# 27 of 35 weight units of two layers multiplied as high and low parts

## What is computed

```
def first_block(x, ...):
    for layer in range(DEPTH):                       # two layers
        h = _rmsnorm(x, norm_g[layer])
        if layer % 2 == 0:
            proj = jnp.einsum('bsd,de->bse', h, e_w_in[i])   # 1024 x 3584
            u_val, u_gate, z_a, q_b, k_b, v_b, z_b = _split(proj, EVEN_SIZES)
            ...
        else:
            proj = jnp.einsum('bsd,de->bse', h, o_w_in[i])
            (q_c, kc_, vc_, ks_, vs_, kw_, vw_, g_c, z_c, q_d, k_d, v_d, z_d) = _split(proj, ODD_SIZES)
            ...
        x = x + jnp.einsum('bse,ed->bsd', y, w_out[layer])
    return x
```

## Time and profile before

| what | value |
| --- | --- |
| time, three runs | 1030.06, 1030.6, 1036.0 us (median 1030.6) |
| the profiled execution | 1030.22 us, of which 1028.4 us are the span of the profile |
| granted TensorE clock, mean | 0.976 |
| PE, busy share | 93% |
| DVE, ACT, POOL, busy share | 35%, 40%, 43% |
| layers 0 and 1 | about 0 to 401 us |
| POOL's first subtraction | 370 us |

### The profile page before, as it was taken

The page is one execution under the profiler, slowest core; times in us unless marked ns, Lnnn a source line. Parts: engine busy times, 40 slices in busy tenths (PEclk is TensorE's granted clock), DMA queues, the critical chain, the costliest instruction groups (busy, mean ns, idle before and its releaser), DMA issues.

```text
span 1028.4 us, 15967 instructions
## 1 busy us (share of the span) xinstructions
PE 957.8 (93%) x6896; PEld 874.2 (85%) x6896; DVE 363.5 (35%) x734; ACT 408.1 (40%) x588; POOL 446.0 (43%) x101
## 2 busy tenths in 40 slices
PE   4999889999898798999999998999999979999996
PEld 4887677788676377999999998999999979999996
DVE  4677521320556626640111113222115643341002
ACT  3111541013576423234343444667533545553330
POOL 0000000000000031787766665766787767886780
PEclk9999899999899999999999998999999989999998
DMA  9632245858524363565534443444544625453531
GB/s 353 257 123 82 83 175 205 329 176 316 196 83 164 124 246 126 175 242 183 185 131 158 158 150 111 160 161 152 177 164 164 238 95 200 168 199 130 204 121 41
DMA packets 27470, 177.51 MB, mean 173 GB/s; under 512 B 2904, under 2 KB 5476, under 8 KB 6920
## 3 DMA queue, kind: packets, MB, share of 16 engines
q1 hardware_dynamic: 25960, 174.28, 46.9%
q10 hardware_dynamic: 1440, 2.20, 0.7%
HBM read 174.88 MB, written 3.43 MB: 173 GB/s over the span
## 4 chain that ended last, share of the span: by engine, by line
PE 84%; DVE 10%; ACT 3%; issue 1%; DMA 1%; POOL 0%; DVEq 0%; ACTq 0%
PE proj L571 18%; PE proj L596 14%; PE proj L597 14%; PE proj L598 14%; PE proj L628 3%; PE proj L630 3%; PE proj L629 3%; PE proj L780 3%; PE proj L617 2%; PE transposed L702 2%; PE proj L810 2%; PE mixed L731 1%; PE scores L690 1%; DVE parts L1561 1%; PE scores L677 1%
## 5 line engine op out<-in xcount | busy, mean ns | idle before, releaser
L521 POOL TENSOR_TENSOR w_lo<-raw,w_hi 128x2048 fp32r<-128x2048 f32 x71 | 329.0, 4639 | 269.7 <-ACT w_hi L1050 269.6
L596 PE MATMUL proj<-parts,w_hi 128*128 128x256 f32 x768 | 222.2, 289 | 6.5 <-DVE parts L1383 4.2
L597 PE MATMUL proj<-parts,w_lo 128*128 128x256 f32 x800 | 227.5, 284 | 0.0
L598 PE MATMUL proj<-parts,w_hi 128*128 128x256 f32 x768 | 218.3, 284 | 0.0
L1050 ACT ACTIVATE w_hi<-raw 128x2048 fp32r<-128x2048 f32 x71 | 135.5, 1909 | 99.4 <-PE proj L598 63.8
L596 PEld LDWEIGHTS proj<-parts,w_hi 128*128 128x128 f32 x768 | 148.1, 193 | 8.1 <-issue 5.2
L597 PEld LDWEIGHTS proj<-parts,w_lo 128*128 128x128 f32 x800 | 154.2, 193 | 0.8 <-issue 0.7
L598 PEld LDWEIGHTS proj<-parts,w_hi 128*128 128x128 f32 x768 | 148.0, 193 | 0.0
L525 POOL MEMSET probT<- 128x512 f32 x1 | 0.5, 525 | 247.8 <-PE proj L897 247.8
L571 PE MATMUL proj<-h,raw 128*128 128x256 f32 x320 | 76.5, 403 | 3.0 <-DVE h L1391 3.0
L571 PEld LDWEIGHTS proj<-h,raw 128*128 128x128 f32 x320 | 64.7, 204 | 14.2 <-issue 4.5
(11 more groups left out here) (273 smaller groups left out, 1940.5 us busy)
## 6 DMA issues: line engine op xcount, KB each, us to landing
raw<-in_weights SPq DMA_DIRECT2D x113, 1024.0 KB, 4.9
arena<-in_weights SPq DMA_DIRECT2D x36, 1024.0 KB, 5.0
probT<-in_weights SPq DMA_DIRECT2D x8, 1024.0 KB, 5.7
dil_lines<-dil_line SPq DMA_DIRECT2D x1, 2304.0 KB, 12.1
dil_bias<-dil_lines SPq DMA_DIRECT2D x1, 1536.0 KB, 9.6
xT<-in_x SPq DMA_DIRECT2D x2, 512.0 KB, 5.6
arena<-in_alibi SPq DMA_DIRECT2D x1, 1024.0 KB, 20.6
arena<-in_swa SPq DMA_DIRECT2D x1, 1024.0 KB, 7.3
```

The lines of the kernel that those rows point to most:

```text
L521: nc.gpsimd.tensor_tensor(lo_slots[RAW_AT[n]][:, 0:kt * w], raw_slots[RAW_AT[n]][:, 0:kt * w], hi_slots[HI_AT[m]][:, 0:kt * w].bitcast(F32 ...
L596: nc.tensor.matmul(dst, whi, h, start=first, stop=False)
L597: nc.tensor.matmul(dst, wlo, h, start=False, stop=False)
L598: last = nc.tensor.matmul(dst, whi, lo[:, k, :], start=False, stop=stop)
```

## The change

Of the 35 units of layers 0 and 1, 27 are now split: all but uv0, ug0, bq1, bk0, bk1, bv0, bv1 and kcvc. For these ACT makes 27 more high copies, and POOL subtracts each in two halves, with one signal behind the second; from rq0 on it subtracts whole units as before. POOL's work for zb0 and what follows waits for `conv_done`, the end of DVE's convolution. The norms of x0 and x1 write whole activations to `h0` and `h1` (`wide`) and then parts: eight ACT copies and eight DVE subtractions each. The attention outputs are split ahead of wo0 and wo1 (`operand_high` on ACT, `parts_low` on DVE; for the first half of wo1 in the fill `Y:c`). The slots of the weights are dealt out anew.

```diff
-SPLIT = WEIGHTS[WEIGHT_AT["rq0"]:]
+WHOLE = ("uv0", "ug0", "bq1", "bk0", "bk1", "bv0", "bv1", "kcvc")
+SPLIT = [u for u in WEIGHTS if u not in WHOLE and u[:2] not in ("ad", "ck", "cv")]
...
-    if u in SPLIT_AT:
+    if u[:4] == "ad10" or u[:3] == "wo1":
+        return EARLY
+    if n >= WEIGHT_AT["rq0"]:
         return range(NRAW + sum(n >= WEIGHT_AT[start] for start in RAW_MORE))
-    return EARLY if n >= WEIGHT_AT["wo1_0"] else [*range(NRAW), *EARLY]
+    return [*range(NRAW), *EARLY[:3 if n >= WEIGHT_AT["wo0_0"] else 2]]
...
-                nc.gpsimd.tensor_tensor(lo_slots[RAW_AT[n]][:, 0:kt * w], raw_slots[RAW_AT[n]][:, 0:kt * w],
-                                        hi_slots[HI_AT[m]][:, 0:kt * w].bitcast(F32), ALU.subtract).then_inc(lo_ready, 1)
-
-            pool.wait_ge(proj_ready, GROUP_AT["hidv"] + 1)
-            nc.gpsimd.memset(probT[:, 0:512], 0.0).then_inc(sem("cmp_zero"), 1)
+                for at in [slice(kt * w // 2 * i, kt * w // 2 * (i + 1)) for i in range(2)] if n < WEIGHT_AT["rq0"] else [slice(0, kt * w)]:
+                    last = nc.gpsimd.tensor_tensor(lo_slots[RAW_AT[n]][:, at], raw_slots[RAW_AT[n]][:, at],
+                                                   hi_slots[HI_AT[m]][:, at].bitcast(F32), ALU.subtract)
+                last.then_inc(lo_ready, 1)
+
             for u in SPLIT:
+                if u == "zb0":
+                    pool.wait_ge(sem("conv_done"), 1)
+                if u == "qd1":
+                    pool.wait_ge(proj_ready, GROUP_AT["hidv"] + 1)
+                    nc.gpsimd.memset(probT[:, 0:512], 0.0).then_inc(sem("cmp_zero"), 1)
                 low(u)
...
             project("uv0", fresh=0)
-            for name in ("ug0", "uv1", "ug1"):
-                project(name)
+            project("ug0")
+            pe.wait_ge(h_ready, KD)
+            project("uv1")
+            project("ug1")
...
-            output(0, "x1", lambda i: plain(f"wo0_{i}", yT0, y_of(0) if i == 0 else None),
-                   lambda i: ada(f"ad{2 + i}"))
+            def gated(layer, i, pieces):
+
+                wait = (lambda k: pe.wait_ge(y_ready, pieces + k // 2 + 1)) if i == 0 else None
+                features(f"wo{layer}_{i}", *h_parts, [[(f"wo{layer}_{i}", P * j, 0)] for j in range(2)], wait)
+
+            output(0, "x1", lambda i: gated(0, i, 0), lambda i: ada(f"ad{2 + i}"))
...
             project("kcvc", fresh=1)
+            pe.wait_ge(h_ready, 2 * KD)
             project("kskw")
...
+            high_parts("x0")
             for i in range(2):
                 copy_out(f"uv{i}", wide[:, 512 * i:512 * i + 512])
...
             attention(PART["b"], FILL_B)
+            passing("wo0_0")
+            operand_high([(hi_of(i), two(yT0, i), [(sem("y_a_ready"), i + 1)] if i < 2 else
+                           [(po_free, 2 * i - 2)]) for i in range(4)])
             table(ACT.Sqrt)
...
             conv_between(PART["b"])
+            parts_low(yT0)
...
             attention(PART["c"] + PART["d"], FILL_CD)
+            parts_low(yT1, range(2, 4))
```

More of the change, by code:

```diff
@@ L365, in mixer_kernel @@
         lo_slots = [w_lo[:, i] for i in range(NRAW)] + \
-            [over("w_lo_a", probT, 0, [P, UNIT])[:], over("w_lo_b", arena, 16384, [P, UNIT])[:]]
+            [over("w_lo_a", probT, 0, [P, UNIT])[:], over("w_lo_b", arena, 16384, [P, UNIT])[:]] + \
+            [over(f"w_lo_e{i}", arena, 4096 + UNIT * i, [P, UNIT])[:] for i in range(len(EARLY))]
         hi_slots = [w_hi[:, i] for i in range(NHI)] + \
@@ L603, in project @@
             def project(name, fresh=None):
[L605 removed]
                 u = UNITS_OF[name][0]
                 if u not in SPLIT_AT:
[L608 to L609 removed]
+                    return plain(name, h0 if name in GROUPS[:GROUP_AT["wo0_0"]] else h1,
+                                 None if fresh is None else lambda k: pe.wait_ge(h_full, KD * fresh + k + 1))
+                wait = None if fresh is None else lambda k: pe.wait_ge(h_ready, KD * fresh + k + 1)
+                features(name, *h_parts, [[(u, P * j, 0)] for j in range(unit_shape(u)[1] // P)], wait)
             def plain_tokens(name, n):
@@ L1012, in _ @@
                     features(name, att_hi, att_lo, [[(f"wa{i // 2}", 256 * (i % 2) + P * j, 0)] for j in range(2)])
-            def merged_product(i):
-                wait = (lambda k: pe.wait_ge(y_ready, 8 + k // 2 + 1)) if i == 0 else None
-                features(f"wo2_{i}", *h_parts, [[(f"wo2_{i}", P * j, 0)] for j in range(2)], wait)
-            output(2, "x3", merged_product, lambda i: None)
+            output(2, "x3", lambda i: gated(2, i, 16), lambda i: None)
             for i in range(16):
@@ L1140, in between @@
                 if "." in name:
+                    return
+                if name[:2] == "Y:":
+                    operand_high([(hi_of(i), two(yT1, i), [(po_free, STEPS_TO["c"])]) for i in range(2)])
                     return
@@ L1285, in _ @@
             attention(PART["c"] + PART["d"], FILL_CD)
+            operand_high([(hi_of(i), two(yT1, i), [(po_free, STEPS_TO["c"] + 2 * i - 2)]) for i in range(2, 4)])
             table(ACT.Sqrt)
@@ L1389, in stream_norm @@
                 for k in range(KD):
-                    dst, made = (h32[:, k, :], h_ready) if n < 2 else (wide[:, S * k:S * k + S], h_full)
-                    V.scalar_tensor_tensor(dst, xT[:, k, :], gain[:, k:k + 1], rstd[:, 0:S], ALU.mult, ALU.mult).then_inc(made, 1)
-                    if split and k >= 2:
+                    dst = h0[:, k, :] if n == 0 else wide[:, S * k:S * k + S]
+                    V.scalar_tensor_tensor(dst, xT[:, k, :], gain[:, k:k + 1], rstd[:, 0:S], ALU.mult, ALU.mult).then_inc(h_full, 1)
+                    if shift is not None and k >= 2:
                         low(k - 2)
-                if split:
-                    low(KD - 2)
-                    low(KD - 1)
+                if name != "xf":
+                    for k in range(KD if shift is None else 2):
+                        low(k if shift is None else KD - 2 + k)
                 V.tensor_copy(bn[:, 0, 9:10], rstd[:, 0:1]).then_inc(norm_done, 1)
```

83 lines of the change are left out of this document (52 added, 31 removed).

## The result

The changed kernel takes 1056.9 us in the median of four runs (1053.5 to 1060.7), the kernel before 1031.7 beside it: a ratio of 1.0239, 95% interval 1.019 to 1.0287. The forecast was 1040 with a range of 1021 to 1050. The profiled execution took 1057.43 us, its span 1055.6.

What follows compares the result with a forecast made beforehand. The prediction took PE, busy 93% of the span, as the bound. Six places, +4.9 +6.3 +1.9 -6.6 +6.8 -3.7, summed to +9.6 us on 1030.2, about 1040 us, range 1021 to 1050.

Steps and rivals of the forecast that it cites:

- What a split unit gives: PE in layers 0 and 1: a full unit falls from 6.91 to 5.76 us; 27 split units save 30.2 us.
- Place 1: Up to the first scores (uv1, ug1, bq0): POOL's lock slows DVE and delays bq0, net +4.9 us.
- Places 2 and 3: First attention, ACT held by wo0_0's load, +6.3; wo0_0 to wo0_3, PE waiting for DVE, +1.9; together +8.2 us.
- Place 4: kcvc to the second attention: PE dense, gain 7.7, 1.1 charged for copies in front of outputs, net -6.6 us.
- Place 5, the nine halves: Second attention: nine halves gain 5.2, 1.8 charged for three high copies and the lock, net -3.4 us.
- Place 5, unit 13: End of second attention: ACT waits for wo1 loads, then DVE subtracts twice under POOL's wo1_1, +10.2 us.
- Place 6: wo1: gain 4.6, the first sums' 1.85 wait goes, wo1_3 waits 2.8 for its low part, net -3.7 us.
- After rq0: The rest of the kernel, from 401 us on, keeps its work: 0 us.
- (a): Rival, whole kernel: PE's saving arrives, 1003 us, or 1013 with half of ACT's waits; chance 13%.
- (b): Rival, whole kernel: ACT waits, but the lock between POOL and DVE costs little, 1024 us; chance 22%.
- (c): Rival: POOL falls behind in place 4, 1047 us, or 1052 with upper ends of places 2 and 3; chance 15%.

Runs made afterwards that it cites:

- e_order: The changed kernel with the same work but ACT's high copies reordered behind exponentials and outputs, and `Y:c` moved to unit 14: 1032.5 us, ratio 1.0014.
- e_wo1_whole: e_order_start with wo1_0 to wo1_3 whole too and y in layer 1 not split: 1027.1 us, ratio 0.9961.
- e_halves_all: e_wo1_whole with POOL's subtractions from rq0 on in halves too: 1020.8 us, ratio 0.9899.
- e_order_start: e_order with uv1, ug1 and bq0 whole and zc0's high copy right behind the squares of qd0: 1027.8 us, ratio 0.9963.
- e_before_8: The kernel before the change with POOL's subtractions in eighths and nothing else changed: 1045.0 us, ratio 1.0131.
- set 4: Two kernels: e_wo1_whole with halves from rq0 on for all units (1020.8 us) or only for wo2, f1_14, f1_15, f2_0 and part of f2_1 (1022.4 us).
- e_eighths: The changed kernel with POOL's subtractions in layers 0 and 1 cut in eight pieces instead of two: 1047.4 us, ratio 1.0157.
- e_in_one: The changed kernel with POOL's subtractions in layers 0 and 1 as whole instructions instead of halves: 1063.5 us, ratio 1.0302.

## Why the prediction was wrong

The direction and both mechanisms were right, the size was not: +9.6 forecast, +27.2 found. By its steps:

- **What a split unit gives.** Between 5.76 us per full unit, as said, and 5.93 (zc0, 266.74 to 272.67). One term had the wrong sign: vdgt. Its 32 records in the type float32 took 4.21 us, its 48 products of 152 columns take 5.41, 113 ns each where 256 columns take 120. I had taken 0.8 gained and bounded it by 0; it is 1.2 lost. Windows over exactly this unit, before (length, PE's busy time and records, and so on as in the earlier trace rows):

```profile
231.82:236.03 4.21, 4.21 (x34) 4.21 (x34) 0.37 (x2) 1.27 (x3) 0.00 (x0) 1.00 0.72 249
```

and in the changed kernel:

```profile
241.73:247.14 5.41, 5.41 (x51) 5.41 (x50) 2.32 (x3) 1.39 (x3) 1.67 (x1) 1.00 0.53 194
```

- **Place 1** (+4.9; found +4.3): right, by its mechanism. bq0 begins at 50.1 where 51.4 was forecast.
- **Places 2 and 3** (+8.2; found +10.3): right by mechanism. The load of wo0_0 landed 7.9 us behind the end of zb1 (7.5 forecast; the two medians in the earlier trace rows are those of two groups of slots, not of a first and a second load). The wait at the transpose grew by 9.5 (9.0 forecast), the entry of wo0 waits 4.82 (5 forecast). The rest is small waits and clock in between. e_order shows that ACT's order carries it: with the same units split, these places give 4.4 us.
- **Place 4** (-6.6; found -0.8): the first step that failed. "I charge 1.1 for copies in front of outputs" names no row, and overlooked that one of these copies, zc0's, stands 6.08 us for its load, the very mechanism that I charged in places 2 and 5. Between 256 and 267 us of the changed kernel 4.9 us are lost by the two waits shown and by the products behind them, which ran at the lower level of the clock (granted 0.50 from 262 to 266.5, 1.2 of 2.4 GHz). With vdgt's 2.0, less the 1.1 charged, that is the 5.8 that the term was off. Mending it took more than moving the copy: where it goes behind the outputs, the low part comes late (e_order), and the time moved only in versions that hit the gap between (-3.9 in e_wo1_whole and e_halves_all, -1.0 in e_order_start). What decides between those two is open beyond the clock, which behind the same wait of 1.62 us was granted 1.00 in e_wo1_whole (242.0 to 244.5) and 0.50 in e_order_start (242.9 to 248.3).
- **Place 5, the nine halves** (-3.4; found +0.4): the charge of 1.8 for the lock and three copies was 3.8 too small. One row of it: PE waits 1.88 us for `prob` at 301.14 where it did not wait before, since the DVE operation of 297.75 took 3.33 us (1.22 when free). An attention in which PE waits for DVE at many units gives little of PE's saving on; the 3.8 were not taken apart further.
- **Place 5, unit 13** (+10.2; found +15.2): the second step that failed, in its size. ACT's part, charged by the landing of the loads, came (the first wait grew from 0.76 by 4.3). "DVE must then subtract twice under POOL's wo1_1" counted two holds. Of the five operations that DVE then had in its queue four were held, three of them tiny, since POOL had four halves queued back to back: 4.7 on the next wait. On the one after it is 2.0, for `prob`, held by the halves of wo1_2 (3.23 us where the kernel before has 1.22). The remaining 4 us are products at a granted clock of 0.50 (378 to 380 and 386 to 389.7; 1.00 in the kernel before), which I charged in places 1 and 3 and not here. How much of these 4 the waits of the change cause is open: behind ad8 e_before_8 and e_wo1_whole lose 4.2 and 3.3 us without such waits.
- **Place 6** (-3.7; found -2.7): right in mechanism. The wait of 1.85 is gone, wo1_3 waits 1.60 for its low part (2.8 forecast).
- **After rq0** (0; found +0.5): right in sum for the change, and in part luck. Where DVE stands to POOL in the MLP shifts with all that lies ahead, and the medians of set 4 show 5 to 6 us that hang on it.

Of the 17.6 us that the forecast lacked, place 4 has 5.8 and place 5 has 8.8. In the main the wrong step is the same in both: the costs of ACT's wait for a load and of POOL's hold were counted for the instructions that looked worst and not for all that stood in the queue.

Of the rivals, (a) is what the mended kernels come towards (1020.8 at best), (b), a cheap lock, did not happen: eighths in place of halves win 9.5 us, and (c), POOL behind in place 4, did not happen there: POOL waited for ACT. It did happen behind rq0 with eighths. Three sums of the forecast are slightly off, and nothing hangs on it: (a) adds up to 1002 and the upper end of (c) to 1053, and bq0's delay is 4.5 us by its own terms. The Trainium skill, page "SBUF — State Buffer" (Who interferes with whom), has the lock last for the whole instruction. By that the halves bound each wait at 2.3 us, and e_eighths, the change and e_in_one agree with 0.76, 2.3 and 4.4. The bound was right and was multiplied by too few operations.

## What to carry to other kernels

A wait in an in-order queue is priced by what the instruction waits for and by everything queued behind it, not by its own duration: list every copy that can reach the head of the queue before its load, not only the two that look worst. Where POOL and DVE share a stretch, count DVE's operations of the held kind under each run of POOL instructions and multiply by the length of one POOL instruction, small operations first; the best size depends on which side is short. From rq0 on halves were best (1020.8 us against 1027.1 whole), and eighths cost 10 to 14 us, since POOL came too late. In layers 0 and 1 of the change, where POOL has more room, eighths took 1047.4 against 1056.9 with halves. Splitting products for PE pays where PE is what everyone waits for; next to an attention put the copies behind its exponentials, and leave units whole whose low parts fall under DVE's busiest stretch.
